# Sixteen modulation tiles computed one stage later, weight parts allocated per stage, and a pad that moves SBUF addresses

## What is computed

```python
for l in range(DEPTH):                               # DEPTH = 2
    mod = jax.nn.silu(c) @ p['w_ada'] + p['b_ada']   # (9, 1024) @ (1024, 6*1024)
    sh1, sc1, gt1, sh2, sc2, gt2 = jnp.split(mod, 6, axis=-1)
    h = rmsnorm(x, p['norm1_g']) * (1.0 + sc1[:, None]) + sh1[:, None]
    mo, st = mixer(h, states, lb_all[l], p)          # HGRN2 | RG-LRU | gated DeltaNet
    x = x + gt1[:, None] * mo
    h = rmsnorm(x, p['norm2_g']) * (1.0 + sc2[:, None]) + sh2[:, None]
    x = x + gt2[:, None] * peer(h, ...)              # product keys, 16384 experts
y = rmsnorm(x, final_norm_g)
```

## Time and profile before

| | |
|---|---|
| median of 3 runs | 2373.83 us (2369.66 to 2375.55) |
| the profiled execution, its own time | 2368.92 us |
| its span in the profile | 2366.9 us |
| PE busy | 2266.2 us (96% of the span) |
| DVE, ACT, POOL busy | 1494.1, 1268.8, 1054.6 us |
| mean granted TensorE clock | 0.97 |
| read from HBM | 449.37 MB |

### The profile page before, as it was taken

One profiled execution on the slowest core, in us unless ns is written; L12 is line 12 of the kernel. 1 busy time (PEld: TensorE's weight loads), 2 busy tenths in 40 slices (PEclk: granted clock), 3 DMA queues, 4 the chain that ended last, 5 costly groups with the idle time before them and its releaser, 6 DMA issues. The chain is left out here.

```text
span 2366.9 us, 58299 instructions
## 1 busy us (share of the span) xinstructions
PE 2266.2 (96%) x20478; PEld 2076.5 (88%) x20478; DVE 1494.1 (63%) x3095; ACT 1268.8 (54%) x2439; POOL 1054.6 (45%) x960
## 2 busy tenths in 40 slices
PE   6989999999999999999999799999999999999998
PEld 4955869999998799999989367799999978999997
DVE  3746636963225968888666664299432288787885
ACT  3533215567557955555556322165665587555554
POOL 0010106884446746566300210088644475665661
PEclk8978999999999999999999779999999999999999
DMA  7475034555552079899545821455555502898992
GB/s 281 155 280 201 3 131 164 178 181 202 188 189 92 6 264 312 287 301 312 194 171 170 310 101 38 137 185 178 199 183 187 188 33 91 295 312 275 312 312 100
DMA packets 123806, 455.40 MB, mean 192 GB/s; under 512 B 13744, under 2 KB 14256, under 8 KB 122544
## 3 DMA queue, kind: packets, MB, share of 16 engines
q1 hardware_dynamic: 105264, 386.80, 45.9%
q0 software_dynamic: 18432, 67.12, 10.3%
HBM read 449.37 MB, written 4.49 MB: 192 GB/s over the span
## 5 line engine op out<-in xcount | busy, mean ns | idle before, releaser
L426 POOL TENSOR_TENSOR parts<-ring,parts 128x512 fp32r<-128x512 f32 x358 | 463.9, 1298 | 472.0 <-ACT parts L419 457.6
L419 ACT ACTIVATE parts<-ring 128x512 fp32r<-128x512 f32 x620 | 389.2, 632 | 348.4 <-PE ps_u L473 280.5
L469 PE MATMUL ps_u<-h_parts,parts 128*128 128x256 f32 x4096 | 563.5, 280 | 0.9 <-ACT parts L419 0.6
L2649 PE MATMUL ps_y<-act_parts,parts 128*128 128x256 f32 x4096 | 563.0, 279 | 0.0
L469 PEld LDWEIGHTS ps_u<-h_parts,parts 128*128 128x128 f32 x4096 | 514.4, 188 | 3.1 <-ACT parts L419 1.7
L2649 PEld LDWEIGHTS ps_y<-act_parts,parts 128*128 128x128 f32 x4096 | 515.1, 188 | 0.7 <-ACT parts L2589 0.3
L426 DVE TENSOR_TENSOR parts<-ring,parts 128x512 fp32r<-128x512 f32 x262 | 180.6, 692 | 372.8 <-ACT parts L419 351.1
L2698 POOL TENSOR_TENSOR act_parts<-big,act_parts 128x256 fp32r<-128x256 f32 x256 | 246.5, 963 | 304.4 <-ACT act_parts L2678 304.4
L473 PE MATMUL ps_u<-h_parts,parts 128*128 128x256 f32 x2048 | 322.7, 279 | 1.4 <-DVE parts L426 1.1
L2653 PE MATMUL ps_y<-act_parts,parts 128*128 128x256 f32 x2048 | 322.3, 279 | 0.0
L473 PEld LDWEIGHTS ps_u<-h_parts,parts 128*128 128x128 f32 x2048 | 275.2, 188 | 2.2 <-DVE parts L426 1.5
(11 more groups left out here) (398 smaller groups left out, 2813.1 us busy)
## 6 DMA issues: line engine op xcount, KB each, us to landing
ring<-in_stream SPq DMA_DIRECT2D x522, 512.0 KB, 3.4
more_ring<-in_stream SPq DMA_DIRECT2D x126, 512.0 KB, 4.9
extra_ring<-in_stream SPq DMA_DIRECT2D x48, 512.0 KB, 5.8
big<-in_stream SPq DMA_DIRECT2D x16, 512.0 KB, 11.7
out_state_out<-big SPq DMA_DIRECT2D x2, 1440.0 KB, 7.0
big<-in_state SPq DMA_DIRECT2D x2, 1280.0 KB, 10.1
big<-in_mixc SPq DMA_DIRECT2D x2, 1024.0 KB, 7.7
big<-in_spots SPq DMA_DIRECT2D x2, 1024.0 KB, 5.5
```

The lines of the kernel that those rows point to most:

```text
L419: eng.activation(m.parts[:, q % PARTS, 0, :], half_tile(m, t, half), ACT.Copy).then_inc(s["hi_ready"], 1)
L426: eng.tensor_tensor(m.parts[:, q % PARTS, 1, :], half_tile(m, t, half), m.parts[:, q % PARTS, 0, :].bitcast(F32), ALU.subtract).then_inc(m ...
L469: pe.matmul(out, hi[:, k, :], hr[:, side, kk, 0:tokens], start=(kk + side == 0), stop=False)
L2649: pe.matmul(ps[:, half * KD // 2 + k, :], hi[:, k, :], act_parts[:, j % AHEAD, side, :], start=False, stop=False)
```

## The change

Tiles 32 to 47 of each layer go from hgrn into gates. Local does 8 tiles instead of 16, hgrn 24 instead of 32. In gates, SP loads the 16 tiles into a ring of three (`mod_ring`), PE multiplies one after each third group (groups 1, 4, ... 22 and 33, 36, ... 54) and turns a section after groups 26 and 58, and ACT copies rows and columns between groups. PE's loop over the groups is written out in full, and the picks are spread two groups ahead through two PSUM banks instead of three through four; the bank freed takes the modulation. The bias and the gain of the two moved sections are now added by DVE in combine, behind the sample tokens' residual. `parts` is allocated by the three stages that use it, behind `big`, and `line_end`, 32 bytes, stands behind `small`. With it every buffer starts at a multiple of 64 bytes.

```diff
 SECTIONS = (3, 4, 2, 5, 0, 1)
-MODS_T = len(SECTIONS) * KD
-LOCAL_ADA = 16
+MODS_T = 4 * KD
+NEXT_T = len(SECTIONS) * KD - MODS_T
+LOCAL_ADA = 8
...
-        self.parts = sb("parts", [P, PARTS, 2, D // 2], F32R)
+        self.parts = None
         self.keep = sb("keep", [P, KEEP_W])
         self.small = sb("small", [P, SMALL_W])
+        self.line_end = sb("line_end", [P, 8])
...
 local_block, tensor:
             turn(0)
-            ada(KD, 2 * KD)
-            turn(1)
 local_block, scalar:
             copy_columns(act, m, s, ps_mod, 0, 1)
-            copy_rows(act, m, s, rows, ps_mod, 1)
-            copy_columns(act, m, s, ps_mod, 1, 2)
 hgrn_block, scalar:
             mask_v(0)
             mask_v(1)
-            copy_rows(act, m, s, ada_rows, ps_mod, 3)
-            copy_columns(act, m, s, ps_mod, 3, 2)
+            copy_rows(act, m, s, ada_rows, ps_mod, 2)
+            copy_columns(act, m, s, ps_mod, 2, 2)
             mask_v(2)
             mask_v(3)
-            copy_rows(act, m, s, ada_rows, ps_mod, 4)
-            copy_columns(act, m, s, ps_mod, 4, 3)
             mask_v(4)
-            copy_rows(act, m, s, ada_rows, ps_mod, 5)
-            copy_columns(act, m, s, ps_mod, 5, 4)
+            copy_rows(act, m, s, ada_rows, ps_mod, 3)
+            copy_columns(act, m, s, ps_mod, 3, 3)
 hgrn_block, tensor:
-            ada(16, 22)
+            ada(8, 14)
             distance(0)
             distance(1)
-            ada(22, 24)
+            ada(14, 16)
             turn(1)
-            ada(24, 26)
+            ada(16, 18)
...
             for d in range(2, C):
                 distance(d)
-                if d == 5:
+                if d == 6:
                     turn(2)
-                ada(*((26, 28), (28, 30), (30, 32), (32, 33), (33, 35), (35, 37))[d - 2])
+                ada(*((18, 20), (20, 21), (21, 22), (22, 24), (24, 25), (25, 26))[d - 2])
...
-            ada(37, 40)
+            ada(26, 28)
             products(2)
             read_states(0)
             products(3)
-            turn(3)
             read_states(1)
-            ada(40, 44)
+            ada(28, 32)
             sample_products()
             read_states(2)
-            ada(44, 48)
+            turn(3)
             mm = read_states(3)
             mm.then_inc(s["inter_ready"], 1)
-            turn(4)
 delta_block, vector:
-                            add_bias(link, m, 0, 6 * KD, m.par("b_ada"))
+                            add_bias(link, m, 2 * KD, 6 * KD, m.par("b_ada")[:, 2 * KD:])
                         elif lv == 4:
-                            norm_gain(link, m, 0)
                             norm_gain(link, m, 1)
 gates_block:
+    BANKS = 2
+    MOD_RING = 3
+    MOD_AT = [1 + 3 * n for n in range(KD)] + [33 + 3 * n for n in range(KD)]
+    MOD_TURNS = (26, 58)
...
+        @block.sync
+        def _(sp):
+            for n in range(NEXT_T):
+                if n >= MOD_RING:
+                    sp.wait_ge(s[f"mod_done{n % MOD_RING}"], n // MOD_RING)
+                sp.dma_start(mod_tile(n), stream[l, T_NEXT + n, :, :]).then_inc(s[f"mod_loaded{n % MOD_RING}"], 16)
...
+            def spots(q):
+                pe.wait_ge(s["first_ready"], q + 1 + SETS - BANKS)
...
+            def gates(q):
+                pe.wait_ge(s["weighted"], q + 1)
+                pe.wait_ge(s["first_ready"], q + 1 + SETS)
+                pe.wait_ge(s["second_ready"], q + 1)
...
+            def modulation(n):
+                if n == KD:
+                    pe.wait_ge(s["cols_out"], 1)
+                pe.wait_ge(s[f"mod_loaded{n % MOD_RING}"], 16 * (n // MOD_RING + 1))
+                ada_product(pe, m, n % KD, mod_tile(n), ps_next).then_inc(s[f"mod_done{n % MOD_RING}"], 1)
+
+            for q in range(BANKS):
+                spots(q)
+            for q in range(GROUPS):
+                if q + BANKS < GROUPS:
+                    spots(q + BANKS)
+                gates(q)
+                if q in MOD_AT:
+                    modulation(MOD_AT.index(q))
+                elif q in MOD_TURNS:
+                    n = MOD_TURNS.index(q)
+                    pe.wait_ge(s["rows_out"], n + 1)
+                    ada_turn(pe, m, ps_next, mod_rows).then_inc(s["cols_ready"], 1)
...
+            def next_rows(n):
+                last = (n + 1) * KD - 1
+                act.wait_ge(s[f"mod_done{last % MOD_RING}"], last // MOD_RING + 1)
+                act.activation(mod_rows, ps_next[:, 0:2 * P], ACT.Copy).then_inc(s["rows_out"], 1)
+
+            def next_columns(n):
+                act.wait_ge(s["cols_ready"], n + 1)
+                dst, src = ada_columns(m, SECTIONS[MODS_T // KD + n], ps_next)
+                act.activation(dst, src, ACT.Copy).then_inc(s["cols_out"], 1)
+
+            onehots(0, 3)
+            next_rows(0)
+            onehots(3, 4)
+            next_columns(0)
+            onehots(4, 7)
+            next_rows(1)
+            onehots(7, TURNS)
+            next_columns(1)
 combine_block, vector, behind the samples' residual:
+            scale, shift = m.mod[:, KD:2 * KD, :], m.mod[:, 0:KD, :]
+            biased = steps(v.tensor_tensor(scale, scale, spread(m.par("b_ada")[:, KD:2 * KD], 2, 1 + NB), ALU.add))
+            v.tensor_tensor(shift, shift, spread(m.par("b_ada")[:, 0:KD], 2, 1 + NB), ALU.add)
+            steps.wait(biased)
+            v.scalar_tensor_tensor(m.gain[:, 0, :, :], scale, 1.0, spread(m.par("norm1"), 2, 1 + NB), ALU.add, ALU.mult)
 build:
-            with nc.sbuf_tensor("x_parts", [P, 2, KD, NT], F32R) as hr:
+            with weight_parts(nc, m, "in_parts"), nc.sbuf_tensor("x_parts", [P, 2, KD, NT], F32R) as hr:
...
-            with nc.sbuf_tensor("h_parts", [P, 2, KD, NP], F32R) as hr:
+            with weight_parts(nc, m, "u_parts"), nc.sbuf_tensor("h_parts", [P, 2, KD, NP], F32R) as hr:
...
-            combine_block(nc, m, l, stream, u_rows)
+            with weight_parts(nc, m, "v_parts"):
+                combine_block(nc, m, l, stream, u_rows)
```

More of the change, by code:

```diff
@@ L67 @@
 T_X = T_V + NKEYS
-TILES = T_X + EXTRAS
+T_NEXT = T_X + EXTRAS
+TILES = T_NEXT + NEXT_T
 SCRATCH_AT = 88
```

71 lines of the change are left out of this document (34 added, 37 removed).

## The result

The changed kernel takes **2390.86 us** (median of 6 runs, 2383.89 to 2393.52), the kernel before 2372.75 in the same comparison (6 runs, 2362.79 to 2375.55). The ratio is **1.0074**, 95% interval 1.0057 to 1.0091: slower by 18 us. The forecast was 2356, faster by 17. The profiled execution took 2393.52 us, with a span of 2391.5 against 2366.9 before.

The account below looks back on a forecast made before the run. PE, busy for 96% of the span, was taken as the bound. Gains of 13.4, 4.5 and 6.4 us less 7.2 lost in gates gave 17.1: from 2373.8 to 2356.7, say 2356 us; range 2346 to 2366, chance 0.58.

Parts of the forecast that it names:

- The addresses: Matmuls of the two large stages: new buffer offsets taken as zero effect, with up to 123 us of gain left open.
- Rival 1: Two large stages: alignment gains 2 to 10 ns in each of 12288 matmuls, 25 to 123 us; chance 0.14.
- Rival 2: Gates takes the moved work in full: 14 us on top of 7, about 2370 us, no change; chance 0.14.
- Rival 3: Gates: PE's written-out program is too long, instruction fetches lose 10 to 48 us, near 2387 us; chance 0.06.
- Local: Section 1 of the modulation leaves local, whose end becomes DVE's last work: 6.5 + 6.9 = 13.4 us gained.
- Hgrn up to the turned keys: First part of hgrn: tiles taken away save nothing more, because POOL's chain is the cover.
- Turned keys to first products: In hgrn, some 13 us in place of 15.6; 2.2 us a layer, 4.5 us gained.
- Hgrn's end: Five tiles fewer are worth 2.2 to 4.3 us a layer; taken as 3.2, twice: 6.4 us gained.
- Gates, PE: The 16 tiles hide at full clock; only slow first groups of layer 0 cost, 1.2 us.
- Gates, ACT: ACT is the bound; copies and waits in its queue cost 1.5 us a section, 3.0 us a layer.
- Delta, output: Delta gains at most 0.4 us a layer, combine's added DVE work costs nothing to 0.6; the two cancel.

Follow-up runs that it names:

- the address part alone: Kernel before plus `line_end` and `parts` allocated per stage right ahead of the moving operand (distance 0), no tile moved: 2412.62 us, ratio 1.0171.
- without the pad: Changed kernel less the `line_end` line, distance from weights to moving operand still 0: 2392.08 us, ratio 1.0083.
- the pad alone: Kernel before with only the `line_end` line added, distance from weights to moving operand 64 bytes: 2375.27 us, ratio 1.0003.
- the run without the copies: Changed kernel with 32 bytes between weights and moving operand; gates without ACT's row and column copies and PE's turns, tiles kept: 2346.20 us, ratio 0.9899.
- the late row copies: Changed kernel with 32 bytes between weights and moving operand; in gates ACT copies each section's rows two groups later: 2347.46 us, ratio 0.9886.
- the run with 160 and 224 bytes: Changed kernel with 160 bytes in the u stage and 224 in the v stage between weights and moving operand: 2371.76 us, one run.

## Why the prediction was wrong

**The addresses: the step that failed.** It read "I take zero, by the nearest row that compares the two offsets", and "from the other side, a loss, the same rows give no sign". The rows compared a VectorE operand at two places; what moved was PE's moving operand against its weights. The term was +35 us in this trace, and 39 us by the run of the address part alone (2412.62 − 2373.60). The 10 ns above 107 that the earlier trace rows left unexplained were rightly seen as open in PE alone, but the bound was drawn on one side, as a gain, though a time that is not at its floor can rise as well as fall. The step also looked only at how far each buffer stands from a multiple of 64, while the change altered something that no single address tells: it put parts and moving operand at the same place modulo 256. That much could be worked out from the allocation beforehand, though nothing in the trace said that it mattered. Of the page cited there (the Trainium skill, Advanced Engine Details and Errata, SBUF Cachelines) the runs say this: with 16-byte lines a start at 32 or 64 ought to be the same, and at an equal distance the place was indeed without effect (1.320 us for twelve matmuls in the changed kernel and without the pad, 1.295 with the pad alone and with 64 bytes between); but the distance between the two is not covered by that rule, and the measurement decides.

**Rival 1** (the alignment is worth a gain) had the right place and the wrong sign for this change; a gain of that kind is there at another distance, 192 bytes: 22.8 us by the medians (2347.46 − 2324.70), 21.0 when each is taken against the kernel before in its own comparison. **Rival 2** saw that PE would be late, with a spacing of 1.4 us between groups; it was 4.00 / 3 = 1.33, and the price 1.0 us a layer where the rival had 7. **Rival 3**, the only slower one, got the side right and nothing else: the run without the copies bounds the written-out program together with the tiles at 1.0 us a layer, and the queue that fetches instructions brought 78 packets for 72. The prediction names two ranges, 2346 to 2366 for the forecast and then 2312 to 2369; 2391 us is the slow side, to which it gave 0.08.

**The rest of the sum.** With the distance restored and all else left as changed, the kernel takes 2356.02 us, 16.9 under the kernel before in its comparison (2372.95); the forecast was 2356, a gain of 17.1. That they agree within 0.2 us is luck: the interval of that run, 0.9912 to 0.9955, stands for 11 to 21 us, and the single steps miss in both directions. By steps, in the changed kernel's trace:

- *Local*: 6.3 and 5.8 us for 6.5 and 6.9, with DVE last. Right, 1.3 us too high.
- *Hgrn up to the turned keys*: nothing saved, 177.40 − 159.78 = 17.6 us against 182.39 − 164.6 = 17.8; POOL's chain is the cover, as said.
- *Turned keys to first products*: 12.8 us, 13 forecast. Right.
- *Hgrn's end*: the stage lost 6.5 us in layer 0, so 3.6 behind the first products, for 3.2. In layer 1 the stage lost 8.5, but there the kernel before was slow in this execution: 65.2 us at a clock of 0.82, where the pad alone and the address part alone, whose hgrn is the same, took 61.8 and 61.4. Some 3.5 of the 8.5 us are thus no work of the moved tiles.
- *Gates, PE*: that the tiles hide is right but for 1.0 us a layer; how they hide is not. "A tile costs 0.43 us every third group, and PE recovers 3 x 0.17 = 0.51 us" fails: a tile takes 4.00 − 3 x 1.11 = 0.67 us. The next pick product starts 0.57 us after the tile and not 0.43, and its weight load waits for DVE's one-hot (line 2569), a wait that the prediction put at nothing. (Whether four PSUM banks would save it was not tried.) So PE does not catch up between tiles but falls back 0.16 us with each, 1.3 us over the eight of a section, and the play of four sets, put at 1.2 us, takes up nearly all of it: ACT keeps its 1.28 us for twenty groups.
- *Gates, ACT*: the mechanism was right, the size too small: 4.6 us a layer for 3.0 (and 1.2 once), of which the late row copies give 3.2 back. The wait for the last tile, put at 0.7 us, was 1.66: ACT had ended its last group at 769.16 − 1.66 = 767.50, and PE, late by its tiles, began the last one only at 768.45. The late copies took that wait away.
- *Delta, output*: −2.6 and +8.6 us. The +8.6 is no cost of moving tiles: the run of the address part alone has the same +8.6 in layer 1 and nothing in layer 0, while the run with 32 bytes between has +0.8. Nor does it need a distance of 0: the pad alone, at 64, takes the same 149.3 us for the two stages in layer 1, and so does layer 0 of the run with 160 and 224 bytes. The mean granted clock of the two stages is 0.90 in all of these and 0.95 where they take 141 us. Why the clock is lower in some executions stays open.
- *Project*: +1.5 and +0.2 us; with 32 bytes between it is 96.2 and 96.3 us, as before. There the columns are 1152 bytes apart, so the distance changes with each.

**What stays open.** Why a distance gives the pace it gives, and which of two rhythms a stretch falls into; no run looks inside PE. That the writers of the parts have no share was tried in the u stage at a distance of 0 alone. Distances of 80, 112 and 144 bytes were not tried, and those other than 0, 32, 64 and 192 rest on one execution each.

## What to carry to other kernels

When a change moves buffers, write down the distance between the two operands that TensorE reads at the same time, not only each one's alignment, and compare a dozen matmuls in both traces before anything else: 3.3 ns in each of 12288 was more than the whole gain of the moved work, and some bytes of padding between the two were worth more than the change itself. A matmul that runs 10 ns above its floor, with a cause unknown, has a price on both sides. And a copy put into the queue of the engine that sets the pace costs its wait more than its work: put it where what it waits for has been done for a group or two, without making the engine before it late.

## What the runs showed of the hardware

- Back-to-back float32r matmuls of 256 columns, each with a weight load, took 113.4 to 120.4 ns at full clock by the distance between weights and moving operand modulo 256 bytes: 120.0 at 0 and near it at 96, mostly 116.4 to 117.0 at 32, 117.7 at 64, 113.4 or 117.7 at 192. Neither operand's own place mattered at 0, 32 and 64, each tried in two placements. The weight loads were reported at 192 ns at 0 and at 187 to 189 at every other distance, at 96 too, so they do not follow the pace.
- The pace has a memory: at 192 bytes one layer of the v stage kept to 117.7 ns and the other to 113.4; at 16 bytes one layer ran mostly at 120.0 and the other did not. A single profile therefore does not show all that such a kernel can do.
